# Seven products in place of eight for three u panels of the short convolution's input projection, in a two-block model kernel

## The chip, the cores and the metric

The kernel runs on one core of one Trainium2 chip (trn2). The metric is the device time of one execution in microseconds (us); lower is better. The median of three runs of the kernel before is 1630.1 us.

## The reference

The reference is a small hybrid language model for one sequence: 16 meta tokens and 512 tokens, 1024 channels, all in fp32. It has an attention layer, an MLP, a short convolution layer, a second MLP and a final hybrid mixer. Both MLPs and the convolution layer are touched by the change:

```python
def short_conv_mixer(h, w_in, conv_w, w_out):
    z = h @ w_in                              # 1024 -> 3 * 1024
    gate_b, gate_c, u = jnp.split(z, 3, axis=-1)
    g = gate_c * u
    y = lax.conv_general_dilated(g, conv_w[:, None, :], ...)   # causal, depthwise, width 3
    return (gate_b * y) @ w_out

def sq_relu_mlp(h, w_up, w_down):             # 1024 -> 4096 -> 1024
    return jnp.square(jax.nn.relu(h @ w_up)) @ w_down

for layer in range(2):
    hn = rms_norm(h, g_mix[layer])
    h = h + (attention_mixer(hn, ...) if layer == 0 else short_conv_mixer(hn, w_in_conv, conv_w, w_out_conv))
    h = h + sq_relu_mlp(rms_norm(h, g_mlp[layer]), w_mlp_up[layer], w_mlp_down[layer])
```

## The kernel before

**Precision.** Every fp32 product is made of three matmuls on numbers cut in two: `hi` (rounded, by ScalarE) and `lo` (the rest, by VectorE). For a weight tile the cut is `split_hi` on ACT (L453) and `split_lo` on DVE (L460); the matmuls are hi x hi, hi x lo and lo x hi (L483).

**Panels and tiles.** Weights come by DMA in panels of 1024 rows and 256 columns into `raw`, which has two halves; panel p goes into half p % 2 and may start when the panel two before it has been cut (`load_panel`, L444, issued by SP in the order of the program). A panel holds two tiles of 128 output channels, numbered through the whole program by t. A tile's result lies in a pair of PSUM banks, `t % 2`, as two halves of 258 tokens. TensorE (PE) starts tile t when its `lo` weights are there (`w_lo_ok`) and when tile t-2 has been taken out of its banks by DVE (`evicted`).

**The convolution's input projection** (`conv_pe`, `conv_act`, `conv_dve`) has four blocks; each is one C panel and one u panel, so four tiles: 96 matmuls of 258 columns for each panel. Below, tile 0 to 3 are those of the first block, tile 4 and 5 are the C tiles of the second. DVE takes each tile out of PSUM, times the norm's scale (L1960), and in the same pass cuts the weights of the tile two ahead (L460). After tiles 2 and 3 it also multiplies C by u (L1967) and applies the three filter taps (L1973, L1976); these four operations are called a set of taps below. The norm's scale is made by ACT after tile 0 (L497, L498), and DVE waits for it before it takes out tile 0.

**Seven products.** From their third panel on (`PLAIN` = 2) the MLPs' up panels are already made by a Strassen-like scheme: rows (tokens) and columns are cut in halves and seven products of 4 x 3 matmuls replace the eight that a plain panel has, 84 matmuls in place of 96 (`product_pe`, L1650). For this

- the activations' halves are mixed once for each norm: ACT scales two chunks into `x_f` (L1546), DVE makes four sums in place (L1555 to L1561), ACT rounds (L1567, `xm_hi`), DVE subtracts (L1573, `xm_lo`). There are four such rounds, and all go through the one buffer `x_f`, so that round i+1 starts when `xm_lo` of round i is done;
- GpSimd (POOL) makes four sums of the panel's weights (L1537, `sw_sum`), and ACT and DVE cut four parts (L1514, L1524: `prep_act`, `prep_dve`);
- ACT copies three products out of PSUM (L1727: `s1`, `s7`, `s6`), and DVE adds the results up (`add_products`, L1798 to L1814) and scales them (L1821).

The order of all work is written out by hand, for each engine, and the engines meet at semaphores.

## Time and profile before

| what | value |
|---|---|
| runs | 1629.82, 1630.1 and 1634.45 us, median 1630.1 us |
| the profiled execution's own time | 1630.15 us |
| its span (first to last instruction) | 1628.4 us |
| PE matmul busy | 1598.7 us, 98% of the span |
| DVE busy | 1016.4 us, 62% |
| ACT busy | 725.8 us, 45% |
| POOL busy | 271.0 us, 17% |

The profiled execution's own time is 1.75 us over its span, and it lies on the median of the runs. All times below are microseconds from the start of the span. Matmuls overlap in the records (a row of the trace says 0.28 us for one), so the pace of PE is read from the length of a long row, not from the mean of one matmul.

### The profile page before, as it was taken

The page shows a single profiled execution, that of the slowest core. Times are in us where ns is not written, and L with a number is a line of the kernel's source. Part 1 is how long each engine was busy: PE and PEld are TensorE (multiplying, and loading weights), DVE is VectorE, ACT ScalarE, POOL GpSimd, SP SyncE. Part 2 cuts the span into 40 slices and gives each one's busy share as a digit, 9 for nine tenths or more (in the row PEclk, how much of TensorE's full clock was granted, in tenths as well). Part 3 has the DMA queues.
Part 4 walks back from the last instruction along what each step waited for, and adds up shares of the span by engine and source line. Part 5 has one row for each costly group of instructions (what it writes and reads, how often), then busy time and mean ns, then how long its engine had stood idle before and what let it go on. Part 6 is the DMA issues. An engine that isn't in the chain of part 4 may idle for free.

```text
span 1628.4 us, 29172 instructions
## 1 busy us (share of the span) xinstructions
PE 1598.7 (98%) x12203; PEld 1417.2 (87%) x12203; DVE 1016.4 (62%) x1416; ACT 725.8 (45%) x1144; POOL 271.0 (17%) x222
## 2 busy tenths in 40 slices
PE   8999999999999999999999999999999999989998
PEld 7998677899999999999887898888887788667896
DVE  6534666388666666555557867677756547856544
ACT  5533554465444444331235544444445445675323
POOL 1002212132222222110004222222212000000200
PEclk9999999999999999999999999999999999999999
DMA  6231030123332222232232333222256676001001
GB/s 197 78 78 31 22 84 10 54 78 130 104 104 89 94 84 99 84 99 93 88 104 78 130 104 104 96 90 100 97 103 99 118 96 89 19 1 62 28 28 52
DMA packets 122689, 134.29 MB, mean 82 GB/s; under 512 B 18877, under 2 KB 99508, under 8 KB 122564
## 3 DMA queue, kind: packets, MB, share of 16 engines
q1 hardware_dynamic: 122362, 132.44, 29.7%
q8 instruction: 93, 1.52, 0.4%
q14 instruction: 32, 0.26, 0.0%
q10 hardware_dynamic: 202, 0.06, 0.0%
HBM read 126.13 MB, written 2.10 MB: 79 GB/s over the span
## 4 chain that ended last, share of the span: by engine, by line
PE 91%; DVE 4%; ACT 2%; issue 1%; DMA 1%; SPq 1%; ACTq 0%; DVEq 0%
PE ps L483 30%; PE ps L1703 22%; PE ps L1650 17%; PE ps L2699 2%; PE ps L829 2%; PE ps L1674 2%; PE ps L812 2%; PE ps L939 1%; PE ps L1220 1%; PE ps L2427 1%; PE ps L837 1%; PE ps L3224 1%; PE ps L2871 1%; PE ps L2850 1%; PE ps L2866 1%
## 5 line engine op out<-in xcount | busy, mean ns | idle before, releaser
L453 ACT ACTIVATE w_hi<-raw 128x1024 fp32r<-128x1024 f32 (+2 forms) x171 | 179.4, 1051 | 400.4 <-PE ps L483 249.4
L483 PE MATMUL ps<-x_hi,w_hi 128*128 128x512 f32 (+4 forms) x872 | 245.8, 333 | 0.5 <-DVE x_lo L503 0.4
L483 PE MATMUL ps<-x_lo,w_hi 128*128 128x512 f32 (+4 forms) x872 | 239.7, 326 | 0.0
L483 PE MATMUL ps<-x_hi,w_lo 128*128 128x512 f32 (+4 forms) x872 | 239.1, 325 | 0.0
L460 DVE TENSOR_TENSOR w_lo<-raw,w_hi 128x1024 fp32r<-128x1024 f32 (+2 forms) x171 | 206.5, 1222 | 45.1 <-ACT w_hi L453 45.1
L1703 PE MATMUL ps<-a_hi,w_hi 128*128 128x258 f32 (+1 forms) x768 | 204.2, 320 | 0.3 <-DVE h L1887 0.3
L1703 PE MATMUL ps<-a_hi,w_lo 128*128 128x258 f32 (+1 forms) x768 | 204.1, 320 | 0.0
L1703 PE MATMUL ps<-a_lo,w_hi 128*128 128x258 f32 (+1 forms) x768 | 204.0, 320 | 0.0
L483 PEld LDWEIGHTS ps<-x_hi,w_hi 128*128 128x128 f32 (+2 forms) x872 | 145.4, 187 | 19.2 <-issue 3.1
L483 PEld LDWEIGHTS ps<-x_lo,w_hi 128*128 128x128 f32 (+2 forms) x872 | 144.6, 186 | 16.4 <-issue 2.2
L483 PEld LDWEIGHTS ps<-x_hi,w_lo 128*128 128x128 f32 (+2 forms) x872 | 144.6, 187 | 14.7
L1537 POOL TENSOR_TENSOR sw_sum<-raw 128x512 f32<-128x512 f32 x56 | 73.5, 1334 | 412.3 <-DMA raw<-in_w_mlp_up 408.6
L1703 PEld LDWEIGHTS ps<-a_hi,w_hi 128*128 128x128 f32 x768 | 127.4, 189 | 11.2 <-issue 0.7
L1703 PEld LDWEIGHTS ps<-a_hi,w_lo 128*128 128x128 f32 x768 | 127.3, 189 | 11.1
L1703 PEld LDWEIGHTS ps<-a_lo,w_hi 128*128 128x128 f32 x768 | 127.7, 189 | 10.7
L1650 PE MATMUL ps<-xm_hi,sw_lo 128*128 128x258 f32 (+1 forms) x448 | 126.6, 283 | 0.0
L1650 PE MATMUL ps<-xm_lo,sw_hi 128*128 128x258 f32 (+1 forms) x448 | 126.6, 282 | 0.0
L1650 PE MATMUL ps<-xm_hi,sw_hi 128*128 128x258 f32 (+1 forms) x448 | 126.1, 281 | 0.0
L1887 DVE TENSOR_TENSOR h<-h,ps 128x516 f32<-128x516 f32 (+1 forms) x128 | 87.8, 686 | 60.5 <-PE ps L1703 60.3
L1727 ACT ACTIVATE s<-ps 128x258 f32<-128x258 f32 (+1 forms) x84 | 32.2, 385 | 140.1 <-PE ps L1650 140.1
L1650 PE MATMUL ps<-x_lo,sw_hi 128*128 128x258 f32 (+1 forms) x336 | 94.5, 281 | 0.0
L1650 PE MATMUL ps<-x_hi,sw_hi 128*128 128x258 f32 (+1 forms) x336 | 94.3, 281 | 0.0
(489 smaller groups left out, 3343.2 us busy)
## 6 DMA issues: line engine op xcount, KB each, us to landing
raw<-in_w_mlp_up SPq DMA_DIRECT2D x32, 1024.0 KB, 5.3
raw<-in_w_mlp_down SPq DMA_DIRECT2D x32, 1024.0 KB, 5.0
raw<-in_w_in SPq DMA_DIRECT2D x16, 1024.0 KB, 9.6
raw<-in_w_in_conv SPq DMA_DIRECT2D x12, 1024.0 KB, 5.0
raw<-in_w_in_attn SPq DMA_DIRECT2D x8, 1024.0 KB, 5.2
raw<-in_w_out_attn SPq DMA_DIRECT2D x4, 1024.0 KB, 5.0
raw<-in_w_out_conv SPq DMA_DIRECT2D x4, 1024.0 KB, 4.9
raw<-in_w_out SPq DMA_DIRECT2D x4, 1024.0 KB, 5.8
```

The lines of the kernel that those rows point to most:

```text
L453: act.activation(split_tile(w_hi, t), raw_tile(t), ACT.Copy).then_inc(w_hi_ok, 1)
L460: dve.tensor_tensor(lo, raw_tile(t), hi.bitcast(F32), ALU.subtract).then_inc(w_lo_ok, 1)
L483: ins = pe.matmul(tile_banks(t)[0:m, b, 0:c], w[:, k, :], x[:, k, x0:x0 + c], start=(k == order[0] and n == 0), stop=(k == order[-1] and n ...
L812: ins = pe.matmul(slot[0:nq, x, c0:c0 + nk], q, k, start=(n == 0), stop=(n == last))
L829: ins = pe.matmul(slot[0:nk, x, c0:c0 + nq], k, q, start=(n == 0), stop=(n == last))
L1537: pool.tensor_tensor(dst, a, b, ALU.add).then_inc(summed, 1)
L1650: ins = pe.matmul(bank, a[:, w, :], b, start=(k == 0 and j == 0 and m in (1, 2, 7, 5)), stop=(k == 3 and j == 2), skip_group_check=m in (6 ...
L1674: ins = pe.matmul(plain_banks(MLP_T0[layer], u, y)[:, bank, 0:c], split_tile(a, t)[:, k, :], b[:, k, nm.first + x0:nm.first + x0 + c], sta ...
L1703: ins = pe.matmul(pair_of_banks[2 + x][:, b, 0:c], split_tile(wt, t)[:, k, P * x:P * x + P], act_in[:, a, x0:x0 + c], start=(k == 0 and j ...
L1727: act.activation(dst[:, 0:hw], ps[:, P_BANK[m], 0:hw], ACT.Copy).then_inc(copied, 1)
L1887: ins = dve.tensor_tensor(like(dst, nm.width), like(dst, nm.width), in_psum(pair_of_banks[2 + x], nm.width), ALU.add)
L2699: ins = pe.matmul(half_tile_banks(q), w[:, k % 4, P * x:P * x + P], a[:, k, 0:SEQ], start=(k == rows[0] and n == 0), stop=(k == rows[3] an ...
```

## The change

1. In blocks 1 to 3 of the convolution's input projection the u panel is made of seven products, the C panels stay plain. The first block stays plain as a whole. The weights of the u panels are summed by POOL, cut in four parts, and so on, as in the MLPs; their products lie in banks 4 to 6.
2. The mixed halves of the activations are made for this norm too (`cm_hi`, `cm_lo`), in the first block, one round before each of its four tiles.
3. The loops over blocks (`Fori(1, 4)` on PE and ACT, `Fori(0, 4)` on DVE) are written out.
4. In all panels of seven products (28 in the MLPs, 3 new ones) the order of the products changes from 1, 5, 7, 2, 6, 3, 4 to 1, 7, 6, 2, 5, 4, 3. Product 1 is copied by ACT from bank 0 into bank 1, and the matmuls of product 2 add to it there; products 6, 5 and 3 add up in bank 0, 4 on 7 in bank 2. So two of DVE's sums and one of its two scalings go away.
5. In the first panel of seven products of each MLP, ACT makes its copies ahead of the cuts for the next panel.

The core of the diff:

```diff
-        s1, s7, s6, s75 = [at(n, t_off + 1056 * i, [P, HW]) for i, n in enumerate(("s1", "s7", "s6", "s75"))]
+        cm_hi, cm_lo = [at(n, a_off + i * 16 * HW * 4, [P, 4, 4, HW], F32R) for i, n in enumerate(("cm_hi", "cm_lo"))]
+        s7, s6 = [at(n, t_off + 1056 * i, [P, HW]) for i, n in enumerate(("s7", "s6"))]
...
-        ORDER = (1, 5, 7, 2, 6, 3, 4)
+        ORDER = (1, 7, 6, 2, 5, 4, 3)
-        P_BANK = {1: 0, 6: 0, 2: 1, 7: 2, 4: 2, 5: 3, 3: 3}
+        P_BANK = {1: 0, 6: 0, 5: 0, 3: 0, 2: 1, 7: 2, 4: 2}
...
             if m == 6:
                 pe.wait_ge(copied, 3 * n + 1)
                 pe.wait_ge(p_lo, 2 * n + 2)
-            if m == 3:
-                pe.wait_ge(added, 3 * n + 1)
+            if m == 5:
+                pe.wait_ge(copied, 3 * n + 3)
             if m == 4:
                 pe.wait_ge(w_lo_ok, t + 2)
                 pe.wait_ge(copied, 3 * n + 2)
+            if m == 3:
+                pe.wait_ge(added, 2 * n + 1)
...
         def conv_act(act):
             for j in range(4):
+                if j:
+                    mix_hi(act, norm2, j - 1)
+                else:
+                    act.wait_ge(mm_done, T_CONV)
+                mix_made(act, norm2, j)
                 split_hi(act, T_CONV + j + 2)
                 if j == 0:
                     norm_scale(act, norm2)
-            with act.Fori(1, 4) as i:
-                for j in range(4):
-                    split_hi(act, T_CONV + j + 2, 4 * i)
+            mix_hi(act, norm2, 3)
+            for i in range(1, 4):
+                for part in (0, 2, 3, 1):
+                    prep_act(act, CONV, i, part)
+                t = T_CONV + 4 * i + 4
+                split_hi(act, t, free=t - 3)
+                split_hi(act, t + 1, free=t - 2)
+                for which in range(3):
+                    copy_act(act, norm2, CONV, i, which)
...
         def conv_dve(dve):
+            for j in range(4):
+                if j:
+                    mix_lo(dve, norm2, j - 1)
+                mix_dve(dve, norm2, j)
+                if j == 0:
+                    dve.wait_ge(scale_ok, norm2.n + 1)
+                conv_evict(dve, 0, j)
+                split_lo(dve, T_CONV + j + 2)
+                if j >= 2:
+                    dve.wait_ge(evicted, T_CONV + j + 1)
+                    conv_taps(dve, 0, j - 2)
+            mix_lo(dve, norm2, 3)
+            for i in range(1, 4):
+                dve.wait_ge(cv["taps"], 6 * i)
+                prep_dve(dve, CONV, i, 0)
+                conv_evict(dve, i, 0)
+                prep_dve(dve, CONV, i, 2)
+                prep_dve(dve, CONV, i, 3)
+                conv_evict(dve, i, 1)
+                prep_dve(dve, CONV, i, 1)
+                split_lo(dve, T_CONV + 4 * i + 4)
+                split_lo(dve, T_CONV + 4 * i + 5)
+                conv_products(dve, i, "11")
+                conv_products(dve, i, "22")
+                conv_products(dve, i, "21")
+                ...
+                conv_products(dve, i, "12")
+                conv_taps(dve, i, 1)
+                conv_taps(dve, i, 0)
```

Three places of the order show what moves. The first is DVE at the start of the convolution's first block, from its cut of tile 1's weights on. `lat<-ps,scale_bc` takes a tile out of PSUM, `w_lo` is the cut of a weight tile. Before:

```order
L460 TENSOR_TENSOR w_lo<-raw,w_hi 128x1024 [waits w_hi_ready]
L1956 UNCONDITIONAL_BRANCH [waits scale_ready]
L1956 ISA
L1960 TENSOR_TENSOR lat<-ps,scale_bc 128x516 [waits tile_done]
L458 REGISTER_ALU
L460 TENSOR_TENSOR w_lo<-raw,w_hi 128x1024 [waits w_hi_ready]
L1958 REGISTER_ALU
L1960 TENSOR_TENSOR lat<-ps,scale_bc 128x516 [waits tile_done]
L458 REGISTER_ALU
L460 TENSOR_TENSOR w_lo<-raw,w_hi 128x1024 [waits w_hi_ready]
```

And of the change, from the same cut on (its lines are numbered anew):

```order
L469 TENSOR_TENSOR w_lo<-raw,w_hi 128x1024 [waits w_hi_ready]
L1573 TENSOR_TENSOR x_f<-x_f 128x258 [waits halves_made]
L1575 TENSOR_TENSOR x_f<-x_f 128x258 [waits halves_mixed]
L1577 SCALAR_TENSOR_TENSOR x_f<-x_f 128x258 [waits halves_mixed]
L1579 SCALAR_TENSOR_TENSOR x_f<-x_f 128x258 [waits halves_mixed]
L1986 TENSOR_TENSOR lat<-ps,scale_bc 128x516 [waits tile_done,scale_ready]
L469 TENSOR_TENSOR w_lo<-raw,w_hi 128x1024 [waits w_hi_ready]
L1591 TENSOR_TENSOR cm_lo<-x_f,cm_hi 128x1032 [waits halves_hi]
L1573 TENSOR_TENSOR x_f<-x_f 128x258 [waits halves_made]
L1575 TENSOR_TENSOR x_f<-x_f 128x258 [waits halves_mixed]
L1577 SCALAR_TENSOR_TENSOR x_f<-x_f 128x258 [waits halves_mixed]
L1579 SCALAR_TENSOR_TENSOR x_f<-x_f 128x258 [waits halves_mixed]
```

Between one tile and the next, DVE now has a `cm_lo` and four operations on `x_f`, each of which waits for ACT (`halves_made`, `halves_hi`) or for the one before it. In the rounds of tiles 2 and 3 the set of taps stands between the weight cut and the next `cm_lo`, as it stood before behind those tiles.

The second place is ACT at the same point, from the norm's scale on (`x_f` is the scaled copy of two chunks, one operation for each; `w_hi` the cut of a weight tile). Before:

```order
L497 ACTIVATE scale_bc<-ps,t_zeros 128x516 [waits stat_ready]
L498 ACTIVATE scale_bc<-scale_bc 128x516 [waits act_step]
L453 ACTIVATE w_hi<-raw 128x1024 [waits tile_done,w_landed1]
L453 ACTIVATE w_hi<-raw 128x1024 [waits tile_done,w_landed0] x2
L1944 UNCONDITIONAL_BRANCH
L1944 ISA
L452 REGISTER_ALU [waits w_landed1]
L453 ACTIVATE w_hi<-raw 128x1024 [waits tile_done]
```

Of the change:

```order
L506 ACTIVATE scale_bc<-ps,t_zeros 128x516 [waits stat_ready]
L507 ACTIVATE scale_bc<-scale_bc 128x516 [waits act_step]
L1585 ACTIVATE cm_hi<-x_f 128x1032 [waits halves_mixed]
L1564 ACTIVATE x_f<-h,vec 128x516 [waits halves_lo]
L1564 ACTIVATE x_f<-h,vec 128x516
L462 ACTIVATE w_hi<-raw 128x1024 [waits tile_done,w_landed1]
L1585 ACTIVATE cm_hi<-x_f 128x1032 [waits halves_mixed]
L1564 ACTIVATE x_f<-h,vec 128x516 [waits halves_lo]
L1564 ACTIVATE x_f<-h,vec 128x516
```

ACT's cut of the weights for tile 3 and for those after it now stands behind a round of the mixing, and waits with it for DVE's `cm_lo` (`halves_lo`).

The third place is DVE in the first panel of seven products of the first MLP, from its two weight cuts on. `s_104` to `s_107` are the copies of products in SBUF, `tmp` is the result. Before:

```order
L460 TENSOR_TENSOR w_lo<-raw,w_hi 128x1024 [waits w_hi_ready] x2
L1798 TENSOR_TENSOR s_107<-s_105,ps 128x258 [waits product_copied]
L1803 TENSOR_TENSOR tmp<-s_104,ps 128x258 [waits a_lo_ready,product_copied,product_done]
L1808 TENSOR_TENSOR tmp<-s_106,s_107 128x258 [waits a_lo_ready,products_added,product_copied]
L1811 TENSOR_TENSOR tmp<-s_106,ps 128x258 [waits product_done]
L1821 SCALAR_TENSOR_TENSOR tmp<-tmp,scale_bc 128x516 [waits tile_evicted,products_added]
L1814 TENSOR_TENSOR tmp<-s_106,ps 128x258 [waits product_done]
L1821 SCALAR_TENSOR_TENSOR tmp<-tmp,scale_bc 128x516 [waits tile_evicted,products_added]
```

Of the change:

```order
L469 TENSOR_TENSOR w_lo<-raw,w_hi 128x1024 [waits w_hi_ready] x2
L1823 SCALAR_TENSOR_TENSOR tmp<-ps,scale_bc 128x258 [waits a_lo_ready,product_done]
L1827 TENSOR_TENSOR tmp<-s_106,ps 128x258 [waits product_done,product_copied]
L1831 TENSOR_TENSOR tmp<-s_107,ps 128x258 [waits product_done,product_copied]
L1840 SCALAR_TENSOR_TENSOR tmp<-tmp,scale_bc 128x516 [waits products_added]
L1834 SCALAR_TENSOR_TENSOR tmp<-ps,scale_bc 128x258 [waits product_done]
```

Five sums and two scalings have become two sums and three scalings, two of these of half the width and straight from PSUM. The sum at L1827, before which PE may not start product 3, is now the second operation of the panel, and one of its inputs is in PSUM.

## Rows read from the trace of the kernel before

**Rows 1.** The page: PE's busy time and its granted clock by slice

```profile
PE 1598.7 (98%) x12203; PEld 1417.2 (87%) x12203; DVE 1016.4 (62%) x1416; ACT 725.8 (45%) x1144; POOL 271.0 (17%) x222
...
PEclk9999999999999999999999999999999999999999
```

**Rows 2.** The chain that ended last, in order of time: start, us, what

```profile
371.99 10.06 PE ps L1650 x84
382.05 11.53 PE ps L1703 x96
...
705.88 174.07 PE ps L483 x1092
```

**Rows 3.** Windows: length, busy of PE, PEld, DVE, ACT, POOL, clock, DMA, GB/s

```profile
710.00:880.00 170.00, 170.00 (x1059) 152.97 (x1058) 101.72 (x126) 49.18 (x58) 10.78 (x6) 1.00 0.29 93
915.00:920.00 5.00, 4.67 (x20) 3.51 (x20) 5.00 (x5) 3.17 (x4) 4.66 (x3) 1.00 0.01 4
```

**Rows 4.** Timeline, DVE in the convolution's first block: start, us, what [idle before]

```profile
707.85 0.69 DVE L1960 TENSOR_TENSOR lat<-ps,scale_bc 128x516 f32<-128x516 f32 x1 [6.36 <-ACT scale_bc L498]
708.47 1.22 DVE L460 TENSOR_TENSOR w_lo<-raw,w_hi 128x1024 fp32r<-128x1024 f32 x1
...
711.39 1.23 DVE L460 TENSOR_TENSOR w_lo<-raw,w_hi 128x1024 fp32r<-128x1024 f32 x1 [0.46 <-ACT w_hi L453]
...
717.16 1.23 DVE L460 TENSOR_TENSOR w_lo<-raw,w_hi 128x1024 fp32r<-128x1024 f32 x1 [0.46 <-ACT w_hi L453]
718.30 0.69 DVE L1967 TENSOR_TENSOR lat<-lat 128x516 f32<-128x516 f32 x1
719.20 0.49 DVE L1973 TENSOR_SCALAR z<-lat,vec 128x512 f32 x1 [0.21 <-DVE lat L1967]
719.84 0.75 DVE L1976 SCALAR_TENSOR_TENSOR z<-lat,vec,z 128x512 f32 x1 [0.16 <-DVE z L1973]
...
727.54 0.69 DVE L1960 TENSOR_TENSOR lat<-ps,scale_bc 128x516 f32<-128x516 f32 x1 [0.30 <-PE ps L483]
```

**Rows 5.** Timeline, ACT in the same block: the norm's scale

```profile
706.64 0.64 ACT L498 ACTIVATE scale_bc<-scale_bc 128x516 f32<-128x516 f32 x1
```

**Rows 6.** Timeline, ACT in the first MLP: mixing and a product's copy

```profile
349.99 1.33 ACT L1546 ACTIVATE x_f<-h,vec 128x516 f32<-128x516 f32 x2
353.73 1.07 ACT L1567 ACTIVATE xm_hi<-x_f 128x1032 fp32r<-128x1032 f32 x1 [2.42 <-DVE x_f L1561]
...
397.93 0.39 ACT L1727 ACTIVATE s<-ps 128x258 f32<-128x258 f32 x1 [2.49 <-PE ps L1650]
```

**Rows 7.** Timeline, DVE in the first MLP: mixing

```profile
352.81 0.43 DVE L1559 SCALAR_TENSOR_TENSOR x_f<-x_f 128x258 f32<-128x258 f32 x1
353.27 0.43 DVE L1561 SCALAR_TENSOR_TENSOR x_f<-x_f 128x258 f32<-128x258 f32 x1
354.83 1.23 DVE L1573 TENSOR_TENSOR xm_lo<-x_f,xm_hi 128x1032 fp32r<-128x1032 f32 x1 [1.14 <-ACT xm_hi L1567]
```

**Rows 8.** Timeline, DVE while POOL sums weights

```profile
357.90 1.70 DVE L460 TENSOR_TENSOR w_lo<-raw,w_hi 128x1024 fp32r<-128x1024 f32 x1
359.53 1.80 DVE L1828 TENSOR_TENSOR a_lo<-tmp,a_hi 128x516 fp32r<-128x516 f32 x1
361.25 1.52 DVE L1555 TENSOR_TENSOR x_f<-x_f 128x258 f32<-128x258 f32 x1
...
402.44 0.41 DVE L1811 TENSOR_TENSOR tmp<-s,ps 128x258 f32<-128x258 f32 x1
```

**Rows 9.** Timeline, POOL's sums at the same times

```profile
358.67 3.82 POOL L1537 TENSOR_TENSOR sw_sum<-sw_sum,raw 128x512 f32<-128x512 f32 x2
...
398.18 2.59 POOL L1537 TENSOR_TENSOR sw_sum<-raw 128x512 f32<-128x512 f32 x2 [12.51 <-DMA raw<-in_w_mlp_up]
...
402.40 1.30 POOL L1537 TENSOR_TENSOR sw_sum<-sw_sum,raw 128x512 f32<-128x512 f32 x1 [0.17 <-POOL sw_sum L1537]
```

**Rows 10.** Timeline, DVE's last cut of an up panel

```profile
391.97 0.68 DVE L1524 TENSOR_TENSOR sw_lo<-raw,sw_hi 128x512 fp32r<-128x512 f32 x1
```

More of the change, by code:

```diff
@@ L413, in half_panel, with sums_read @@
             return raw[:, p % 2, 0:KC * PANEL].rearrange("q (k n) -> q k n", k=KC // 2)
+        def sums_read(sp, p):
+            for n, (layer, u) in enumerate(FAST):
+                if tiles[up_tile(layer, u)][0] == p - 2:
+                    sp.wait_ge(summed, 4 * n + 4)
         def load_half_panel(sp, p):
+            sums_read(sp, p)
             free = panels[p - 1]["first"]
@@ L434, in load_panel @@
         def load_panel(sp, p, dt=0, row_shift=0, col_shift=0):
+            sums_read(sp, p)
             if p >= 2:
@@ L1510, in prep_act @@
             if n:
-                before = (layer, u - 1) if u > PLAIN else (0, NU - 1)
-                act.wait_ge(product, max(product_at(*before, m) for m in PART_READERS[part]))
+                act.wait_ge(product, 7 * (n - 1) + max(ORDER.index(m) for m in PART_READERS[part]) + 1)
             dst, src = weight_part(layer, u, part, sw_hi)
@@ L1792, in add_products @@
         def add_products(dve, nm, layer, u, what):
-            n, t, hw = nth_up(layer, u), up_tile(layer, u), nm.width // 2
-            b1, b2, b3 = [ps[:, b, 0:hw] for b in (1, 2, 3)]
-            if what == "75":
-                dve.wait_ge(copied, 3 * n + 2)
-                dve.tensor_tensor(s75[:, 0:hw], s7[:, 0:hw], b3, ALU.add).then_inc(added, 1)
+            n, hw, f = nth_up(layer, u), nm.width // 2, nm.first
+            b0, b1, b2 = [ps[:, b, 0:hw] for b in range(3)]
+            read = FF // P * layer + 2 * u
@@ L1824, in a_low, with scale_dve @@
+        def scale_dve(dve, nm, layer, u):
+            n, w = nth_up(layer, u), nm.width
+            dve.wait_ge(added, 2 * n + 2)
+            dve.scalar_tensor_tensor(tmp[:, 1, 0:w], tmp[:, 1, 0:w], 0.0, scale_bc[:, nm.first:], ALU.min, ALU.mult).then_inc(scaled, 1)
         def a_low(dve, nm, layer, u, tile):
             w, c = nm.width, 2 * u + tile
-            dve.wait_ge(a_hi_ok, FF // P * layer + c + 1)
+            dve.wait_ge(a_hi_ok, FF // P * layer + 2 * u + (tile if u < PLAIN else 1 - tile) + 1)
@@ L3337, in _ @@
             norm_pool(pool, norm2)
+            for u in range(1, 4):
+                for which in range(4):
+                    sums_pool(pool, CONV, u, which)
             mlp_pool(pool, norm3, 1)
```

213 lines of the change are left out of this document (114 added, 99 removed).

## The prediction

> **What bounds the kernel now.** I first read PE's share and clock on the page: PE has matmuls in 98% of the span, and every slice has a full granted clock, so this run is at the upper of the two levels, 2.4 GHz, from end to end [rows 1]. Next the chain that ended last: from the first MLP to the convolution's end it is unbroken PE work, and its pieces give PE's prices. A panel of seven products takes 10.06 us for 84 matmuls, a plain one of the same width 11.53 us for 96; the whole convolution stage is one piece of 174.07 us [rows 2]. Then the windows: from 710 to 880 us PE is busy for 170.00 of 170.00 us while DVE is busy for 101.72 and ACT for 49.18 [rows 3]. So in this stage only PE's own work sets the time. Fewer matmuls are worth their full price, and DVE and ACT have room on the average. An average, though, tells nothing of one block. Last I read DVE's and ACT's timelines where the change puts work in [rows 4 to 9], since the reader should see that the new work stands in a ring between two engines.
>
> **What is taken away.** In three panels 96 matmuls become 84: 3 x (11.53 - 10.06) = -4.41 us [rows 2]. The order of rows shows the 84, so the shortening itself is certain. Writing the loops out costs PE nothing: it had no gap in them [rows 3].
>
> **What the mixing adds, in block 0.** Four rounds of mixing go between tiles 0 to 3. I walk DVE, since PE may not start tile t before DVE has cut its weights and taken out tile t-2. Prices: taking a tile out 0.62 us until the next operation starts (707.85 to 708.47), a weight cut 1.14 until the next and 1.23 to its end (717.16, 718.30) [rows 4]; `x_f` made by ACT 1.33, its rounding 1.07 [rows 6]; each of the four sums 0.46 from start to start, so 1.73 until DVE can go on, and the `lo` 1.23 [rows 7].
>
> - Round 0 is hidden: DVE sat idle for 6.36 us there, waiting for the scale [rows 4], which ends at 706.64 + 0.64 = 707.28 [rows 5].
> - From 707.3 on: tile 0 out, cut for tile 2, and the first `lo` starts at 707.3 + 0.62 + 1.14 = 709.06.
> - A full round is lo 1.23, x_f by ACT 1.33 (DVE waits, since x_f is one buffer), sums 1.73, tile out 0.62, cut 1.14, two hand-overs 0.06: 6.11 us. The second `lo` starts at 715.17. The cut for tile 3 ends at 715.26, and PE wants tile 3 at about 715.75 (5.77 us a tile, and tile 4 ends at 727.5, when DVE takes it [rows 4]). It holds, by half a microsecond.
> - The next round is 6.11 plus the set of taps. That was 0.69 + 0.49 + 2 x 0.75 = 2.68, and gaps of 0.21 and 0.16 in it that belong to the loop's registers [rows 4]; written out I take 2.75 in all. Third `lo`: 715.17 + 6.11 + 2.75 = 724.03.
> - From there lo, x_f, sums, tile 3 out, cut for tile 5 to its end: 1.23 + 1.33 + 0.06 + 1.73 + 0.62 + 1.23 = 6.20, so the weights of tile 5 are ready at 730.2. PE wants them at 727.5 [rows 4].
>
> That is a stall of 2.7 us even if nothing disturbs DVE, and it is one stall, not four: afterwards PE has tile 5 (5.77 us) to run, in which DVE finishes the taps, the last `lo` and the first cut of the u panel. The first cut of the summed weights then comes some 0.1 us late for product 7: +0.1.
>
> **POOL's sums collide with this.** The load of the first fast u panel may start when tile 3's weights are cut, at 715.26. In the MLP it is 5.53 us from the end of such a cut (391.97 + 0.68) to POOL's first sum at 398.18 [rows 9, 10]. So POOL starts at 720.8 and does four sums of 1.3 us, exactly while DVE does the taps. What this costs is to be seen at 358 to 363 us: a cut that takes 1.22 took 1.70, an `a_lo` of 0.70 took 1.80, a sum of 0.43 took 1.52, each ending where one of POOL's two sums had (3.82 us for two of 1.3) [rows 8, 9]. Three operations lost 2.67 us, 0.9 each. A sum whose one input is in PSUM took 0.41 with POOL busy, so it loses nothing [rows 8, 9]. Of the operations behind 720.8 four have both inputs in SBUF (product of C and u, two taps, the third `lo`): 4 x 0.9 = 3.6 us. Walking them in strict turns with POOL (cut for tile 4 ends 721.37, then sum, product, sum, tap, sum, tap, sum) starts the third `lo` at 728.7 instead of 724.03: 4.7 us. I take 4.2, between the two. The stall before tile 5 is then 2.7 + 4.2 = +6.9 us; its ends are 2.7 (no collision) and 7.4.
>
> The Trainium skill, page "SBUF — State Buffer", section "Who interferes with whom", says that a DVE instruction with two SBUF inputs and a GpSimd instruction that reads SBUF exclude each other for a whole instruction. It speaks against this change: by it the 4.7 would hold and the time be 1632.9 us. The rows above show just such turns, but with 0.9 us for each meeting the sum gives 1631.8.
>
> **Blocks 1 to 3.** Behind the end of the previous products DVE has the last take-out (0.42), two sets of taps (5.5), a cut, a tile out and the second cut, 1.14 + 0.62 + 1.23: 8.9 us. Product 7 needs that second cut at 11.53 + 1.44 = 12.97. There are 4.1 us to spare, and POOL's sums fall into this stretch again; four meetings cost 3.6 to 5.2. I take 0, with up to 1.1 us for each of blocks 2 and 3. ACT's part (2 x 1.04 and less) is short. Behind block 3 no sums follow, and the B tiles give DVE 11 us.
>
> **The new order in the MLPs.** One product lasts 10.06 / 7 = 1.44 us. Three new waits of PE: product 6 on the copy of product 1, product 5 on the copy of product 6, product 3 on the sum that reads bank 0 behind product 5. Each has one whole product in between as cover; a copy takes 0.39 [rows 6], a sum 0.41 [rows 8], so each has 1.0 us to spare. No row shows a copy from PSUM into PSUM. Its nearest is the 0.39 into SBUF; it costs nothing until it takes 1.4. In the first panel of each MLP, ACT's two cuts are now behind the copies; DVE's "22" then ends 1.0 us before product 3. So 0. What can be gained is one wait: in the second MLP PE is busy for 4.67 of 5.00 us at 915 to 920, behind the first fast panel [rows 3]. DVE's tail there is shorter by a sum and a scaling: -0.33.
>
> **Sum.** -4.41 + 6.9 + 0.1 - 0.33 = +2.3 us against the profiled execution's 1630.15 (which equals the median of the runs): **1632.4 us**. A difference under 0.3%, 4.9 us, can't be told from no change.
>
> **The rivals.**
> - *The forecast*: one stall of 6 to 7.5 us before tile 5 eats the matmuls' gain: 1631.5 to 1633.5. 0.55.
> - *No collision*: POOL's sums come later, or take their turns without harm. The stall is 2.7: 1630.15 - 4.41 + 2.7 + 0.1 - 0.33 = 1628.2. For it: a load that lands 3 us late is enough. 0.17.
> - *Hidden altogether*: DVE is only 60% busy in the stage [rows 3], and mixing in the first MLP costs PE nothing there. Then -4.74: 1625.4. Against it: there the rounds had no taps between them and a tile pair each. 0.08.
> - *DVE late in blocks 2 and 3 too*: 1.1 each on top of the forecast: 1634.6. 0.12.
> - *Slower, by one mechanism in the products*: if one of the three waits is longer than its cover, PE pays the excess in all 31 panels. At 0.1 us each it decides (2.3 + 3.1 = 5.4 over before, above 4.9); at 0.2 it gives 1638.6. For it: the copy within PSUM has no row. Against it: 1.0 us of cover. 0.08.
>
> **How the numbers follow.** The range has to take in the first, second and fourth: 1627.5 to 1635.5. Faster by over 0.3% (below 1625.2) is about half of the hidden case, 0.05. Slower (above 1635.0) is most of the last case and a part of the fourth, with the forecast's own tail: 0.16. Same: 0.79.
>
> **What would show it.** In the changed profile PE should have one long wait near 728 to 735 us, released by DVE's weight cut; the `cm_lo` rows should start near 709, 715 and 728.7; taps there should take over 1 us where POOL sums. The u panels of blocks 1 to 3 should be 10.06 us long with no wait in them, and the MLPs' panels as before. If PE waits in every panel of seven products for ACT's copy, or if the `cm_lo` rows come 5.8 us apart without a wait behind them, I am wrong.

## The result, and the profile after

| | kernel before | changed kernel |
|---|---|---|
| median, same chip, 12 runs each | 1629.79 us (1628.12 to 1634.45) | 1636.01 us (1632.06 to 1640.39) |
| ratio to before, 95% interval | | 1.0038 [1.0029, 1.0047] |
| the profiled execution | 1630.15 us | 1637.51 us |
| its span | 1628.4 us | 1635.7 us |

The changed kernel is slower: 6.2 us, 4.7 to 7.7 by the interval. Forecast were +2.3 and a top of the range of 1635.5. Its twelve times fall in two groups: six from 1632.06 to 1634.52 and six from 1637.51 to 1640.39. The profiled execution is of the upper group. Two executions of the kernel before on later chips, of 1729 and 2590 us, were in a slow state and are left out below.

The page of the changed kernel, PE's line and its clock by slice:

```profile
PE 1600.0 (98%) x12167; PEld 1418.9 (87%) x12167; DVE 1000.0 (61%) x1395; ACT 741.5 (45%) x1171; POOL 287.8 (18%) x234
...
PEclk9999999999999999989999999999999999999989
```

There are 36 matmuls fewer than in [rows 1], and PE is busy 1.3 us longer. Fewer matmuls that take longer mean a lower clock, and two digits of the clock line are 8: slice 18 (695 to 736 us), which holds the convolution's first block and the start of tile 5, and slice 39 (1554 to 1595 us) near the end. The chain that ended last, in order of time (start, us, what):

```profile
695.88 7.22 PE ps L492 x60
...
732.22 8.47 PE ps L492 x48
740.69 10.05 PE ps L1668 x84
750.75 11.53 PE ps L492 x96
762.28 10.05 PE ps L1668 x84
...
901.02 5.83 PE ps L1692 x24
```

The one piece of 174.07 us in [rows 2] is broken at 732.22. The three u panels are 10.05 us long, as the sum had them. But tile 5, the piece in front, has 48 matmuls in 8.47 us where tiles of before took 5.77. Why it starts at 732.22 is in PE's timeline, where from 695 to 890 us a single row has a wait (in brackets: idle before, and what ended it):

```profile
732.22 0.80 PE L492 MATMUL ps<-x_hi,w_hi 128*128 128x258 f32 x2 [6.63 <-DVE w_lo L469]
```

And DVE's and POOL's timelines show what DVE did instead of cutting tile 5's weights:

```profile
719.37 1.80 DVE L2013 TENSOR_TENSOR lat<-lat 128x516 f32<-128x516 f32 x1
721.21 1.42 DVE L2015 TENSOR_SCALAR z<-lat,vec 128x512 f32<-128x512 f32 x1
722.67 3.39 DVE L2018 SCALAR_TENSOR_TENSOR z<-lat,vec,z 128x512 f32<-128x512 f32 x2
725.98 1.22 DVE L1591 TENSOR_TENSOR cm_lo<-x_f,cm_hi 128x1032 fp32r<-128x1032 f32 x1
728.61 0.43 DVE L1573 TENSOR_TENSOR x_f<-x_f 128x258 f32<-128x258 f32 x1 [1.41 <-ACT x_f L1564]
...
730.95 1.22 DVE L469 TENSOR_TENSOR w_lo<-raw,w_hi 128x1024 fp32r<-128x1024 f32 x1
732.08 0.69 DVE L2013 TENSOR_TENSOR lat<-lat 128x516 f32<-128x516 f32 x1
732.80 0.49 DVE L2015 TENSOR_SCALAR z<-lat,vec 128x512 f32<-128x512 f32 x1
733.33 1.54 DVE L2018 SCALAR_TENSOR_TENSOR z<-lat,vec,z 128x512 f32<-128x512 f32 x2
```

```profile
718.75 3.60 POOL L1555 TENSOR_TENSOR sw_sum<-raw 128x512 f32<-128x512 f32 x2 [17.99 <-issue]
722.51 1.28 POOL L1555 TENSOR_TENSOR sw_sum<-sw_sum,raw 128x512 f32<-128x512 f32 x1 [0.17 <-POOL sw_sum L1555]
723.97 1.55 POOL L1555 TENSOR_TENSOR sw_sum<-sw_sum,raw 128x512 f32<-128x512 f32 x1 [0.17 <-POOL sw_sum L1555]
```

The same set of taps stands there twice. With POOL's sums beside it, it goes from 719.37 to 725.98, 6.61 us; behind them from 732.08 to 734.78, 2.70. So the collision costs 3.91 us. The row at 728.61 has the other part of the ring: DVE idle for 1.41 us while ACT fills the one buffer `x_f`. Windows (length, busy of PE, PEld, DVE, ACT, POOL, clock, DMA, GB/s):

```profile
725.00:730.00 5.00, 0.59 (x5) 0.38 (x4) 3.49 (x6) 2.29 (x3) 0.51 (x1) 0.75 0.00 0
730.00:735.00 5.00, 2.78 (x13) 2.78 (x14) 4.89 (x8) 4.42 (x5) 0.00 (x0) 0.50 0.31 93
735.00:740.00 5.00, 5.00 (x33) 5.00 (x33) 5.00 (x5) 1.06 (x1) 0.00 (x0) 0.72 0.34 119
...
1565.00:1580.00 15.00, 14.72 (x140) 14.15 (x137) 3.94 (x10) 3.09 (x7) 0.00 (x0) 0.66 0.21 72
```

A granted clock of 0.50 is the lower level, 1.2 GHz; from 730 to 735 us PE was never above it. In the wait the clock fell, and tile 5's matmuls paid for it: 8.47 - 5.77 = 2.70 us. The last window is a second place, some 835 us later, in the final mixer: PE is busy for 14.72 of 15 us, and two thirds of them are at the lower level. What PE did just before the second place are small matmuls; two rows of the changed kernel's timeline:

```profile
1558.18 2.33 PE L2925 MATMUL ps<-gdn_T,gdn_LB 64*64 64x64 f32 x64
...
1562.13 1.13 PE L2946 MATMUL ps<-gdn_TT,gdn_Y 64*64 64x32 f32 x31
```

Two windows of the kernel before belong beside these:

```profile
264.00:272.00 8.00, 6.99 (x83) 4.66 (x85) 7.46 (x14) 4.18 (x9) 2.84 (x4) 0.82 0.01 2
...
1565.00:1580.00 15.00, 15.00 (x151) 14.75 (x149) 5.36 (x17) 6.37 (x11) 0.00 (x0) 1.00 0.21 71
```

At 1565 us the kernel before has the full clock. At 264 it has 0.82, where this execution of the changed kernel has 1.00; its slice still shows a 9, since 9 is everything from 90% up. This stretch changes from execution to execution and not with the kernel: five profiles of this case have 1.00 there and begin the convolution between 695.88 and 696.26 us (this one, `e1_mlp_only`, `e7_mix_only`, `e10_no_ring_again`, `e12_later_yet`), eight have 0.80 to 0.86 and begin it between 697.35 and 697.79 (the two shifted kernels before, `e8_shift_before` and `e11_half_shift`, begin at 697.14 with 1.00 and at 698.49 with 0.84). So two executions can differ by some 1.5 us before the change is reached, and the stage is measured below from its own beginning, the row of 7.22 us, to the opening of the second MLP: 200.25 us in the kernel before.

The two profiled executions then compare like this. The row of 7.22 us with 60 matmuls, the convolution's beginning, starts at 697.79 before and at 695.88 after: -1.91, from the stretch at 264 us and not from the change. The 24 matmuls that open the second MLP start at 898.04 and at 901.02. So the stage of the change costs 2.98 + 1.91 = +4.89 us, and that is -4.41 (three panels) + 6.63 (the wait) + 2.70 (the clock behind it) = 4.92. The last long piece, 8.33 us of 36 matmuls, starts at 1613.79 and at 1621.12: 7.33 later instead of 2.98, so +4.35 behind the second MLP's start, nearly all of it from the second place: the unaltered kernel without the late loss (`e0_again`, below) takes 716.00 us for this stretch, this execution 720.10 and the kernel before 715.75.

### The profile page after: what moved, and what is told of

Read it like the earlier page. It is cut to its first block, busy times and chain, and to the rows that moved or that the text cites. A ratio compares the mean times of both kernels' runs of the same rounds, so it can differ in the third digit from the quotient of the medians.

```text
span 1635.7 us, 29028 instructions
## 1 busy us (share of the span) xinstructions
PE 1600.0 (98%) x12167; PEld 1418.9 (87%) x12167; DVE 1000.0 (61%) x1395; ACT 741.5 (45%) x1171; POOL 287.8 (18%) x234
## 4 chain that ended last, share of the span: by engine, by line
PE 90%; DVE 5%; ACT 2%; issue 1%; DMA 1%; SPq 0%; POOL 0%; ACTq 0%; DVEq 0%
PE ps L492 27%; PE ps L1721 22%; PE ps L1668 19%; PE ps L2774 2%; PE ps L838 2%; PE ps L1692 2%; PE ps L821 2%; PE ps L948 1%; PE ps L1229 1%; PE ps L2502 1%; DVE w_lo L469 1%; PE ps L846 1%; PE ps L3299 1%; PE ps L2946 1%; PE ps L2925 1%
## 5 line engine op out<-in xcount | busy, mean ns | idle before, releaser
L492 PE MATMUL ps<-x_hi,w_hi 128*128 128x512 f32 (+3 forms) x776 | 227.7, 340 | 7.1 <-DVE w_lo L469 6.6
L492 PE MATMUL ps<-x_lo,w_hi 128*128 128x512 f32 (+3 forms) x776 | 221.4, 332 | 0.0
L492 PE MATMUL ps<-x_hi,w_lo 128*128 128x512 f32 (+3 forms) x776 | 220.7, 332 | 0.0
L1555 POOL TENSOR_TENSOR sw_sum<-raw 128x512 f32<-128x512 f32 x62 | 81.9, 1342 | 469.2 <-DMA raw<-in_w_mlp_up 410.0
L492 PEld LDWEIGHTS ps<-x_hi,w_hi 128*128 128x128 f32 (+1 forms) x776 | 131.6, 188 | 26.0 <-DVE w_lo L469 7.1
L492 PEld LDWEIGHTS ps<-x_lo,w_hi 128*128 128x128 f32 (+1 forms) x776 | 130.7, 187 | 16.4 <-issue 2.2
L492 PEld LDWEIGHTS ps<-x_hi,w_lo 128*128 128x128 f32 (+1 forms) x776 | 130.8, 188 | 14.7
L1753 ACT ACTIVATE tmp<-tmp 128x516 f32<-128x516 f32 (+1 forms) x64 | 40.1, 626 | 153.8 <-DVE tmp L1840 150.1
L1668 PE MATMUL ps<-x_lo,sw_hi 128*128 128x258 f32 (+1 forms) x372 | 104.7, 281 | 0.0
L1668 PE MATMUL ps<-x_hi,sw_hi 128*128 128x258 f32 (+1 forms) x372 | 104.6, 281 | 0.0
```

The lines of the kernel that those rows point to most:

```text
L492: ins = pe.matmul(tile_banks(t)[0:m, b, 0:c], w[:, k, :], x[:, k, x0:x0 + c], start=(k == order[0] and n == 0), stop=(k == order[-1] and n ...
L1555: pool.tensor_tensor(dst, a, b, ALU.add).then_inc(summed, 1)
L1668: ins = pe.matmul(bank, a[:, w, :], b, start=(k == 0 and j == 0 and m in (1, 7)), stop=(k == 3 and j == 2), skip_group_check=m not in (1, 7))
L1753: act.activation(tmp[:, tile, 0:w], tmp[:, tile, 0:w], ACT.Square).then_inc(relu_sq, 1)
```

## The experiments

All chips here ran the kernel before beside the experiments; medians and ratios are against those runs. "Theory A" is the account above: a ring of DVE and ACT, collisions with POOL on top, one wait at tile 5, and the clock behind it. "Theory B" is named anew with each experiment. From `e8_shift_before` on, both theories are about the second place alone.

**The changed kernel again, on another chip** (`e0_again`).

> The changed kernel once more, unaltered, to see whether its runs fall into two groups again (six of twelve at 1632.1 to 1634.5 us, six at 1637.5 to 1640.4). Theory A (one wait of PE before tile 5, 6.6 us, and a lower clock behind it, 2.7 us; a second stretch of lower clock late in the program, about 5 us, comes in some executions only): two groups again, some 5 us apart, the lower one 3 to 4 us over the kernel before. Theory B (something else that the change does costs time everywhere): one group, about 6 us over the kernel before.

1634.82 us against 1630.08, ratio 1.0034 [1.0022, 1.0046]. The same wait, but the clock comes back earlier and tile 5 is 7.57 long, 1.80 over 5.77:

```profile
733.73 7.57 PE ps L492 x48
```

```profile
730.00:735.00 5.00, 1.27 (x6) 1.27 (x7) 4.71 (x9) 4.06 (x6) 0.00 (x0) 0.54 0.05 7
735.00:740.00 5.00, 5.00 (x35) 5.00 (x35) 4.96 (x6) 2.47 (x3) 0.00 (x0) 0.77 0.60 204
...
1560.00:1580.00 20.00, 19.51 (x294) 18.69 (x289) 6.21 (x17) 7.64 (x15) 0.00 (x0) 1.00 0.17 55
```

The late loss (the one of the second place) is missing in this profile. Four of its six times lie from 1633.91 to 1635.07, two at 1637.6.

**Only the MLPs' part** (`e1_mlp_only`): the convolution's code as before, the new order of products and copies kept in the MLPs.

```diff
-        FAST = [(0, u) for u in range(PLAIN, NU)] + [(CONV, u) for u in range(1, 4)] + [(1, u) for u in range(PLAIN, NU)]
+        FAST = [(0, u) for u in range(PLAIN, NU)] + [(1, u) for u in range(PLAIN, NU)]
...
-            for u in range(1, 4):
-                for which in range(4):
-                    sums_pool(pool, CONV, u, which)
```

> Only the new order of the products and copies in the MLPs; the convolution is that of the kernel before. Theory A: the order costs nothing and takes one wait of 0.33 us away: within 1 us of the kernel before, none of the 28 panels longer than 10.06 us. Theory B (the copy within PSUM or the new waits cost in every panel, or the new order lowers the clock later on): at least 3 us over the kernel before.

1628.74 us, ratio 0.9994 [0.9985, 1.0003]: no change that can be measured, so the loss comes with the convolution's part. In the changed kernel ACT's copy from PSUM into PSUM, the operation without a row, took less than the one into SBUF:

```profile
742.17 0.37 ACT L1741 ACTIVATE ps<-ps 128x258 f32<-128x258 f32 x1 [0.32 <-PE ps L1668]
743.62 0.39 ACT L1741 ACTIVATE s<-ps 128x258 f32<-128x258 f32 x1 [1.07 <-PE ps L1668]
```

**PE kept busy in the wait** (`e2_keep_busy`): 28 matmuls of the identity into bank 7, which nothing reads, before tile 5.

```diff
                 for j in range(4 if i == 0 else 2):
+                    if 4 * i + j == 5:
+                        keep_busy(pe, ps[:, 7, :], 28)
                     dense_tile(
```

> The changed kernel with 28 matmuls of 128x128 whose result nobody uses put before tile 5, about 6.0 us at 0.21 each, so that PE is busy in most of its wait. Theory A: the weights of tile 5 come no earlier, so it starts at the same time, but the clock stays at its upper level and tile 5 takes 5.8 us in place of 8.5: 2.7 us faster than the changed kernel run beside it. Rival (tile 5 was slow for another reason, such as its operands being written at that time): no change.

1630.93 us, ratio 1.0013 [1.0002, 1.0024]. Against the changed kernel unaltered on the same chip this is 3.9 us less, though DVE is no faster and tile 5 starts at the same time. Chain and window:

```profile
733.78 6.04 PE ps L492 x48
...
739.82 10.13 PE ps L1668 x84
```

```profile
730.00:735.00 5.00, 4.63 (x41) 4.44 (x40) 4.65 (x9) 4.07 (x6) 0.00 (x0) 1.00 0.04 8
```

With the clock at 1.00, tile 5 takes 6.04 instead of 7.57. The clock's price is shown: 1.5 us between these two traces. The medians differ by more than that, and the late loss can't be the rest: without the three of these eleven times that are high (1635.26 to 1636.89) and the two of the six, the medians are 1630.90 and 1634.28, still 3.4 us apart. The stretch at 264 us and a longer fall of the clock in other executions of the unaltered kernel could be; no trace of one of the low times here shows it. The profiled execution had the late loss (0.66 at 1565 to 1580 us) though PE idled for no more than 0.37 us before tile 5.

**POOL's first sums later** (`e3_pool_late`): they wait until tile 3 has been taken out.

```diff
+                if u == 1:
+                    pool.wait_ge(evicted, T_CONV + 4)
                 for which in range(4):
                     sums_pool(pool, CONV, u, which)
```

> The changed kernel, but POOL's sums for the first u panel wait until tile 3 has been taken out of PSUM, so that they don't meet the first set of taps. Theory A (meetings with POOL are 3.9 us of the wait): the first set of taps takes 2.7 us instead of 6.5, PE's wait before tile 5 falls from 6.6 to 2.7 or 3, and the clock may hold: 3.6 to 6.3 us faster than the changed kernel beside it, less what the later sums cost product 6 (up to 2 us). Rival (the ring between ACT and DVE is what makes the wait, POOL is innocent): the wait stays above 6 us.

1635.5 us, ratio 1.0027 [1.0017, 1.0037]. PE's waits:

```profile
729.78 0.57 PE L492 MATMUL ps<-x_hi,w_hi 128*128 128x258 f32 x2 [2.72 <-DVE w_lo L469]
738.64 0.39 PE L1668 MATMUL ps<-x_hi,sw_hi 128*128 128x258 f32 x1 [1.32 <-DVE sw_lo L1542]
```

The wait at tile 5 falls from 6.62 to 2.72, the 3.9 of the collision. The second set of taps now collides, and 1.32 comes back at the first u panel. The clock did not hold: it is 0.66 from 730 to 735 us, and tile 5 takes 7.54 us (729.78 to 737.32), 1.77 over 5.77. Behind the wait of 1.32 it is 1.00. The waits alone are 2.6 us shorter, but the median isn't: in six of its nine executions the time lies at 1635.4 or above and in three at 1631.4 to 1632.9. The three are some 2.3 us below the low group of `e0_again`, and the stage is 2.0 us shorter (202.20 against 204.23), so the first place did give something. The profiled execution has the late loss (0.61 at 1565 to 1580 us), and in this program the second place took what the first gave.

**A second buffer** (`e4_two_buffers`): rounds 1 and 3 use a second `x_f`.

```diff
+        x_f2 = at("x_f2", place["tmp"] - 2 * LEN * 4, [P, 4, HW])
+        def mix_buf(nm, i):
+            return x_f2 if nm.n == 2 and i % 2 else x_f
...
+            if nm.n == 2 and i:
+                act.wait_ge(xs["lo"], 4 * g + i - 1)
```

> A second buffer for the mixing's x_f in rounds 1 and 3, so that ACT makes the next rows while DVE still cuts the last ones; all else as in the changed kernel. Theory A (ring of DVE and ACT, then collisions with POOL, then the clock): DVE's 1.4 us idle in front of each round's first sum goes, three times, so PE's wait before tile 5 falls from 6.6 us to about 2.4, tile 5 takes 5.8 to 7.0 us, and the time is 4 to 7 us below the changed kernel's: 1628 to 1631, about the kernel before. Theory B (the wait is DVE's own work and the collisions, ACT not a part of the ring): the wait stays above 6 us and the time at 1634 to 1636.

1629.14 us against 1628.95, ratio 1.0000 [0.9991, 1.0009]. Timeline and chain:

```profile
729.38 0.51 PE L497 MATMUL ps<-x_hi,w_hi 128*128 128x258 f32 x2 [2.31 <-DVE w_lo L474]
```

```profile
729.38 7.55 PE ps L497 x48
```

DVE's three waits of 1.41 are gone and so are 4.3 us of the stall: ACT was part of the ring. What is left, 2.31 us, still cost the clock, tile 5 being 1.78 over 5.77. The account gives -4.41 + 2.31 + 1.78 = -0.32, and the runs say no difference. The changed kernel itself was not run on this chip.

**Tile 5's cut first** (`e5_cut_first`): DVE cuts tile 5's weights ahead of both sets of taps and of the last round.

```diff
-            for j in range(4):
+            for j in range(3):
...
-                if j >= 2:
-                    dve.wait_ge(evicted, T_CONV + j + 1)
-                    conv_taps(dve, 0, j - 2)
+            conv_evict(dve, 0, 3)
+            split_lo(dve, T_CONV + 5)
+            dve.wait_ge(evicted, T_CONV + 4)
+            conv_taps(dve, 0, 0)
+            mix_lo(dve, norm2, 2)
+            mix_dve(dve, norm2, 3)
+            conv_taps(dve, 0, 1)
```

> On DVE tile 3 is taken out and tile 5's weights are cut ahead of both sets of taps and of the last mixing round; nothing is taken away. Theory A (DVE is short of time over the whole of the first block): the wait at tile 5 goes, but the rows cm_lo and the first cut of the summed weights come as much later, and a wait of 4 to 7 us stands in the first u panel at product 1 or 7; the time stays within 2 us of the changed kernel's, 1633 to 1636. Theory B (only the order of DVE's work is at fault; tile 5's 5.8 us are cover enough): no wait over 1 us anywhere and 1626 to 1629.

1632.85 us, ratio 1.0016 [1.0005, 1.0028]. No wait at tile 5, but at the first product of the u panel:

```profile
738.95 0.58 PE L1668 MATMUL ps<-x_hi,sw_hi 128*128 128x258 f32 x1 [5.76 <-DVE sw_lo L1542]
```

```profile
738.95 12.66 PE ps L1668 x84
```

The stall is DVE's total of work up to the summed weights: this order of the same work only moves it. Here the panel pays for the clock, 12.66 - 10.05 = 2.61. Account: -4.41 + 5.76 + 2.61 = 3.96; the stage is 3.90 us longer in the traces (204.15 against 200.25), and the runs say 2.6 (0.8 to 4.6). The profiled execution is the highest of the eleven, 1640.62 us, with the late loss (0.56 at 1565 to 1580 us); the other ten lie at 1632.03 to 1634.78.

**No ring** (`e6_no_ring`): two buffers, and the first block's taps behind cuts of the first u panel, where PE has 84 matmuls to run.

```diff
+                if i == 1:
+                    prep_dve(dve, CONV, 1, 0)
+                    dve.wait_ge(evicted, T_CONV + 4)
+                    conv_taps(dve, 0, 0)
+                    prep_dve(dve, CONV, 1, 2)
+                    prep_dve(dve, CONV, 1, 3)
+                    conv_taps(dve, 0, 1)
```

> Two buffers for x_f as above, and both sets of taps of the first block moved behind cuts of the first u panel, where PE has seven products to run. Theory A: no wait of PE over 1 us from 695 to 890 us, granted clock 1.0 throughout the stage, and the whole gain of the 36 matmuls is seen: conv stage 4.4 us shorter than before, time 1625 to 1627 wherever no low-clock stretch falls late in the program. Theory B (taps only move the stall): a wait of 3 us or more in the first u panel, and 1629 to 1632.

1626.15 us, ratio 0.9984 [0.9975, 0.9993]: faster than both kernels. From 695 to 890 us no row of PE has a wait:

```profile
710.00:880.00 170.00, 169.91 (x1040) 151.80 (x1039) 130.68 (x160) 65.73 (x85) 30.12 (x19) 1.00 0.29 94
```

The second MLP opens at 894.14, in the kernel before at 898.04, with equal beginnings of the convolution (697.74 and 697.79): -3.85 of the -4.41. Of what is missing, 0.20 stands in the second u panel, which took 10.25 us.

**Mixing alone** (`e7_mix_only`): the rounds of the first block are kept, all panels are plain, POOL sums nothing there. `cm_hi` and `cm_lo` are made and not read.

```diff
-                for j in range(4 if i == 0 else 2):
+                for j in range(4):
...
-                if i:
-                    for m in ORDER:
-                        product_pe(pe, norm2, CONV, i, m)
```

> Mixing rounds of the first block kept, but all convolution panels plain again, 96 matmuls each, and no sums by POOL: the rows cm_hi and cm_lo are made and not read. Theory A (ring 2.7, collisions 3.9): the taps take 0.69, 0.49 and 0.75 us again, PE waits 2.7 us before tile 5 and not 6.6; if the clock falls only behind long waits tile 5 takes 5.8 us and the time is 1632.5 to 1633.0, if it falls behind this one too, 1633.5 to 1635. Theory B (the stall comes from POOL alone): no wait, and 1629.5 to 1630.5.

1632.46 us, ratio 1.0025 [1.0016, 1.0034].

```profile
728.39 0.51 PE L492 MATMUL ps<-x_hi,w_hi 128*128 128x258 f32 x2 [2.73 <-DVE w_lo L469]
```

```profile
725.00:730.00 5.00, 2.27 (x15) 2.06 (x14) 4.83 (x9) 2.71 (x3) 0.00 (x0) 0.89 0.08 18
730.00:735.00 5.00, 5.00 (x35) 5.00 (x34) 3.88 (x5) 0.00 (x0) 0.00 (x0) 0.76 0.56 193
```

This is the ring without POOL: 2.73 us, by the prediction's walk 2.7. And even this wait is followed by a lower clock: the stage takes 204.73 us (695.95 to 900.68), 4.48 more than before, so 1.75 on top of the wait. By the ratio the kernel is 4.1 us slower (2.6 to 5.5), by the medians 3.5.

**The late loss: is a later position enough?** (`e8_shift_before`, and later `e11_half_shift`): the kernel before, with 21 or 12 matmuls of the identity before tile 4.

```diff
                 dense_tile(pe, T_CONV + j, xh, xl, NW, k_ready=hooks.get(j))
+            keep_busy(pe, ps[:, 7, :], 21)
             with pe.Fori(1, 4) as i:
```

> The kernel before with 21 matmuls of 128x128 by the identity into an unused bank before tile 4 of the convolution: PE does 4.8 us of useless work, never idles and keeps its clock there, and all that comes behind is moved by about as much as in the changed kernel. The rest is that of before. The question is the second loss, of about 4 us, that some executions of the changed kernel had at 1560 to 1580 us with a granted clock near 0.7. Theory A (the later position in the program is enough): 1634.6 to 1635.1 for most executions and 1638 to 1640 for a third or more of them. Theory B (it needs the idle time and the fall of the clock in the convolution): 1634.6 to 1635.1, with no more late losses than the kernel before has, one execution in ten.

1633.06 us, ratio 1.0021 [1.0011, 1.0031]; the added piece was 4.69 us long. Ten times lie from 1632.12 to 1633.88, two at 1635.54 and 1636.75; the granted clock of these two executions, 0.998 and 0.999, is that of the other ten. So at most two of twelve had the late loss, as by Theory B. The low times are 0.7 to 2.5 us below what both theories had expected.

**The changed kernel once more** (`e9_changed_again`) **and the one without the ring** (`e10_no_ring_again`), on the chip of `e8_shift_before`.

> The changed kernel once more, unaltered, for the count of executions with the late loss and as the partner of the next kernel on the same chip. Theory A and B alike: 1632 to 1635 without the late loss and 1637 to 1640 with it; from the 18 executions so far, 8 with it, some 4 of 10 again. If none or all have it, the state of the chip decides and not the kernel.

1634.07 us, ratio 1.0031 [1.0018, 1.0045]: nine times from 1632.41 to 1635.85, three from 1638.78 to 1640.11. The profiled execution (1635.85) has no late loss (1.00 from 1560 to 1580 us). Behind its wait of 6.62 us it has the longest low stretch (0.50 from 730 to 735 and 0.52 from 735 to 740 us), and tile 5 is 2.91 over 5.77:

```profile
733.82 8.68 PE ps L492 x48
```

> The kernel with two x_f buffers and the first block's taps behind the cuts, once more: 1625.0 to 1627.5 in most executions, 7 to 9 us below the changed kernel on this chip, 2 to 4 us below the kernel before; the profile again without a PE wait from 695 to 890 us.

1625.45 us against 1629.45, ratio 0.9977 [0.9968, 0.9986]. The gain of `e6_no_ring` came again, and the changed kernel lies 8.6 us above it on this chip. The profile has no wait of PE from 695 to 890 us, and the stage takes 196.38 us (696.19 to 892.57), 3.87 less than before.

**The kernel before with 12 matmuls of the identity** (`e11_half_shift`), the edit of `e8_shift_before` with a smaller number.

> The kernel before with 12 useless matmuls of 128x128 before tile 4 of the convolution, where the earlier kernel had 21: 2.7 us of PE work, no idle time, no fall of the clock there. The profiles with the late loss so far had the first products of the second MLP between 899.5 and 901.9 us, the nine without it at 892.6 to 898.1, at 902.1 and 902.9, and two inside the band. This kernel puts it at 899 to 901. Theory A (the late loss depends on where in the program's time the stage of small matmuls falls): a third or more of its executions are 4 us or more above the others, which lie at 1630.5 to 1633. Theory B (the changed kernel's own work or its idle time brings it): one in ten, and a median of 1632.

1636.18 us, ratio 1.0026 [1.0011, 1.0041]. Its twelve times fall in five from 1631.04 to 1633.78 and seven from 1635.72 to 1639.07, as by Theory A. The seven have a granted clock of 0.996 or 0.997 over the whole execution, the five 0.998 or 0.999, so the seven did lose clock somewhere; the profiled execution is one of the five and has 1.00 at 1560 to 1580 us. 12 useless matmuls are 2.68 us, and the median rose by 6.8: more than with 21. The kernel before beside it had 4 high times (1633.8 or above) in 21. It has no wait and no change of the clock in the convolution, so high times of this size need neither. Whether it is the later position or the added matmuls themselves that brought them, these runs don't tell apart.

**The changed kernel pushed further back** (`e12_later_yet`): as `e2_keep_busy`, with 48 matmuls instead of 28.

> The changed kernel with 48 useless matmuls before tile 5 instead of the 28 of the earlier kernel: 11 us of PE work in the place of the wait, 4.6 us more than there, no idle time. The second MLP's first products come at 904 to 905 us. Theory A (position): out of the band, so the late loss is rare, one in ten or fewer, and nearly all executions lie at 1634.5 to 1637.5. Theory B (something in the changed kernel brings the late loss wherever it lies): a quarter to a half of its executions 4 us above the others, at 1639 to 1642.

1635.80 us, ratio 1.0039 [1.0025, 1.0053]: nine times from 1634.53 to 1636.82, three from 1639.11 to 1640.42. The three have a granted clock of 0.996 or 0.997, the nine 0.998 or more. The second MLP opened at 902.59 in the profiled execution, short of the expected 904 to 905 but outside the positions where the late loss had been seen (899.5 to 901.9), and a quarter of the times are high, at 1639 to 1640.4: the numbers of Theory B. Against Theory A in that form stand also three profiles inside these positions without the late loss (`e0_again` 901.62, `e7_mix_only` 900.68, `e11_half_shift` 901.41). For the first place this kernel is the cleanest case: with the wait filled whole, the clock is 1.00 and tile 5 has its full pace.

```profile
725.73 10.72 PE ps L3301 x96
736.45 5.76 PE ps L492 x48
```

## Why the prediction was wrong

**Where and why PE would wait: right, and nearly in size.** The walk along DVE gave one wait before tile 5, released by its weight cut, 6.9 us long, from 2.7 of ring and 4.2 of collision. The traces have 6.63, 2.73 (`e7_mix_only`) and 3.91. The `cm_lo` rows were forecast near 709, 715 and 728.7. With this execution's 1.9 us added they stand at 709.1, 715.2 and 727.9; the third had been walked with strict turns of DVE and POOL, a collision of 4.7 in place of 3.9.

**One rule in it was wrong.** "A sum whose one input is in PSUM took 0.41 with POOL busy, so it loses nothing" was in effect stretched to the first tap, which has one tensor input but in SBUF: only operations with two inputs in SBUF were counted. It took 1.42 instead of 0.49. Four operations collided, as forecast, but not the same four: the product lost 1.11, the first tap 0.93, the two others 1.85 together, and the third `lo`, which had been counted, nothing. The total was right because two errors met. The Trainium skill, page "SBUF — State Buffer", section "Who interferes with whom", says that `tensor_scalar` can enter a mode that uses both port pairs, and then contends with GpSimd. By that sentence the tap can count, and the trace agrees: 1.42 us beside POOL's sums.

**The step that failed is the stall's price in the sum.** "+6.9 us" charged a wait with its length alone; the clock behind it was put at nothing, without a reason. Every wait of 2.3 us or more in the convolution that was profiled was followed by matmuls at the lower level:

| kernel | PE's wait, us | the piece behind it against its length at full clock |
|---|---|---|
| second buffer | 2.31 | 7.55 for 5.77: +1.78 |
| POOL's sums later | 2.72 | 7.54 for 5.77: +1.77 |
| mixing alone | 2.73 | +1.75, by the stage's length |
| changed kernel, second profile (`e0_again`) | 6.62 | 7.57 for 5.77: +1.80 |
| changed kernel, first profile | 6.63 | 8.47 for 5.77: +2.70 |
| changed kernel, third profile (`e9_changed_again`) | 6.62 | 8.68 for 5.77: +2.91 |
| tile 5's cut first | 5.76 | 12.66 for 10.05: +2.61 |

With PE busy in the wait the clock stayed (`e2_keep_busy`; `e12_later_yet`, where tile 5 took 5.76). With the changed kernel's 1.8 to 2.9 in it, the sum is 1634.2 to 1635.3 instead of 1632.4. That is still inside the stated range, and the changed kernel's executions without the late loss lie about it, at 1632.06 to 1635.85 in the three sets of runs. So this term explains how the stage came to +4.89, and the second loss, below, is what took the first median past the top of the range. The prediction read from the clock line of [rows 1] that "every slice has a full granted clock" and the run is at the upper level "from end to end", which its digits can't say: the windows of the same execution have 0.82 at 264 to 272 us. The Trainium skill, page "TensorE: Matmul & The Clock Gate", section "HAM oscillation — how this bites in real kernels", says that a PE which waits between stretches of work is throttled again and starts the next cold; it had been left out, and this case's rows agree with it: behind the wait of 6.63 us the granted clock was 0.50.

**A second loss, of about 4 us, needs no wait in the convolution, and its cause stays open.** The prediction had no term for it. It lies at 1560 to 1580 us in some executions: by the gap in the times, in 11 of 30 of the changed kernel (6 of 12, 2 of 6, 3 of 12); these have a granted clock of 0.993 or 0.994, the other 19 of 0.995 to 0.998. The kernel before had 12 of 120 times at 1633.8 or above. What is shown: it comes with a lower clock there, and it occurs with the clock at 1.00 and no wait over 0.37 us in the convolution (`e2_keep_busy`). From the second MLP's opening to the last long piece of PE it is 719.74 to 722.39 us in the four profiles with it and 715.15 to 716.58 in the eleven without it; between two profiles of the changed kernel it costs 4.10. The kernel before with 2.7 us of useless matmuls has high times in 7 of 12. None of these seven was itself profiled; that they are the same loss is argued from their size and their clock. What stays open: why 4.7 us of the same brought at most 2 of 12, and the changed kernel, moved by about as much, more; and whether the chip has a share. On the chip of `e4_two_buffers` to `e7_mix_only` 1 of 22 executions of `e5_cut_first` and `e7_mix_only` had it by the same gap, with their profiles opening the second MLP at 901.87 and 900.68, but the changed kernel was not run there. So the first median, 1636.0, holds a share of this: its six low times have a median of 1633.4, 3.6 us over before. The medians of the other two sets, 1634.8 and 1634.1, hold less.

**The smaller terms.** 10.05 for the u panels: right. No waits in blocks 2 and 3: right, though taps collide there too (751.30, 1.29 us for the product of C and u instead of 0.69; 752.62, 1.40 us for the first tap). No wait in the 31 panels for copies: right in size, they take 10.06, 10.05 and 9.97 us. In the second MLP the wait of [rows 3] went: PE is busy for 41.62 of the 42 us from 898 to 940 in the kernel before, and for 41.98 of those from 901 to 943 in the changed one. But nothing was gained. The MLP's later panels are a little longer than they were (9.97 us instead of 9.95, and 11.14 instead of 11.11), and from its opening to the next stage's first tile it is 375.19 us before (898.04 to 1273.23) and 375.36 after (901.02 to 1276.38).

## What to carry to other kernels

On a path that one engine's unbroken work sets, a new wait costs its length and what the clock takes from the work behind it, here 1.8 to 2.9 us for waits of 2.3 to 6.6; either fill the wait with matmuls that nobody reads, or remove it whole, since a third of it cost nearly the same clock. When extra work for another engine is put in a tight stretch, walk that engine operation by operation as here, and then look for a place where the bound engine has its longest uninterrupted run: moving two sets of taps by one panel and adding one buffer turned +4.89 us in this stage into -3.85 (medians: +6.2, +4.7 and +4.6 into -2.8 and -4.0). Read the clock in windows of a few microseconds, not in the 40 slices, and where a kernel's times fall in two groups, count the groups before explaining a median.
